# Attention of a hybrid diffusion layer: probabilities computed keys by queries, row sums by ones beside the values, part of the splitting on GpSimd

## The reference, cut to what matters

```python
def one_block(qi):
    s = jnp.einsum("bqkgd,bskd->bkgqs", qi, k).astype(f32) * scale
    p = jax.nn.softmax(s, axis=-1).astype(v.dtype)
    return jnp.einsum("bkgqs,bskd->bqkgd", p, v)
```

## Time and profile before

| what | value |
|---|---|
| median of 3 runs | 2630.91 us (2629.97 to 2631.04) |
| the profiled execution, its own time | 2627.32 us |
| its span, first to last instruction | 2625.6 us |
| PE busy | 2451.6 us, 93% |
| DVE busy | 1925.7 us, 73% |
| ACT busy | 827.6 us, 32% |
| POOL busy | 186.5 us, 7% |
| the attention's loop | from about 1024 to 1299 us of the span |

### The profile page before, as it was taken

The page is one execution under the profiler, slowest core; times in us unless marked ns, Lnnn a source line. Parts: engine busy times, 40 slices in busy tenths (PEclk is TensorE's granted clock), DMA queues, the critical chain, the costliest instruction groups (busy, mean ns, idle before and its releaser), DMA issues. The chain is left out here.

```text
span 2625.6 us, 38449 instructions
## 1 busy us (share of the span) xinstructions
PE 2451.6 (93%) x15508; PEld 1500.0 (57%) x15508; DVE 1925.7 (73%) x2867; ACT 827.6 (32%) x1313; POOL 186.5 (7%) x220
## 2 busy tenths in 40 slices
PE   7999999999999787999799889899899999999987
PEld 2555555555555466777576666545455555555543
DVE  4687777789576766888648658798877676677687
ACT  2411111111121345777644454623222121122220
POOL 0000000000000022222200000311000000000002
PEclk9999999999999889999899999899999999999998
DMA  8133322331212111000120111231211111111001
GB/s 329 49 113 97 97 83 94 97 113 62 67 36 85 63 37 27 1 1 1 31 67 15 42 45 37 69 102 49 65 48 48 48 33 47 48 48 38 26 25 65
DMA packets 151085, 160.55 MB, mean 61 GB/s; under 512 B 11767, under 2 KB 128403, under 8 KB 149922
## 3 DMA queue, kind: packets, MB, share of 16 engines
q1 hardware_dynamic: 150946, 158.61, 19.1%
HBM read 148.47 MB, written 10.12 MB: 60 GB/s over the span
## 5 line engine op out<-in xcount | busy, mean ns | idle before, releaser
L2010 PE MATMUL psum<-act_hi,ffn_win_hi 128*128 128x384 f16 x2064 | 675.2, 327 | 4.8 <-DVE ffn_win_lo L2334 2.4
L2010 PE MATMUL psum<-act_lo,ffn_win_hi 128*128 128x384 f16 x2064 | 674.8, 327 | 0.0
L2010 PE MATMUL psum<-act_hi,ffn_win_lo 128*128 128x384 f16 x2064 | 674.7, 327 | 0.0
L2210 ACT ACTIVATE ffn_silu<-psum,ffn_win_inverse 128x384 f32<-128x384 f32 x132 | 76.3, 578 | 1061.5 <-PE psum L2010 1057.8
L2402 DVE SCALAR_TENSOR_TENSOR Y<-psum,ffn_h_unit,Y 128x512 f32<-128x512 f32 x324 | 239.8, 749 | 108.2 <-PE psum L2055 106.2
L2055 PE MATMUL psum<-ffn_wout_hi,ffn_h_hi 128*128 128x512 f16 x720 | 278.1, 386 | 7.5 <-issue 5.3
L2010 PEld LDWEIGHTS psum<-act_hi,ffn_win_hi 128*128 128x128 f16 x2064 | 202.5, 98 | 139.1 <-DVE ffn_win_lo L2334 2.8
L2010 PEld LDWEIGHTS psum<-act_hi,ffn_win_lo 128*128 128x128 f16 x2064 | 202.5, 98 | 134.7 <-issue 2.0
L2010 PEld LDWEIGHTS psum<-act_lo,ffn_win_hi 128*128 128x128 f16 x2064 | 202.5, 98 | 133.9 <-issue 1.5
L2055 PE MATMUL psum<-ffn_wout_lo,ffn_h_hi 128*128 128x512 f16 x720 | 277.7, 386 | 0.0
L2055 PE MATMUL psum<-ffn_wout_hi,ffn_h_lo 128*128 128x512 f16 x720 | 277.2, 385 | 0.0
(11 more groups left out here) (379 smaller groups left out, 4298.3 us busy)
## 6 DMA issues: line engine op xcount, KB each, us to landing
ffn_win_raw<-in_w_in SPq DMA_DIRECT2D x88, 512.0 KB, 5.1
w_mod<-in_w_mod SPq DMA_DIRECT2D x36, 1024.0 KB, 5.0
ffn_wout_raw<-in_w_out SPq DMA_DIRECT2D x44, 512.0 KB, 4.1
scan_w_raw<-in_w_mix SPq DMA_DIRECT2D x20, 512.0 KB, 5.3
x_after<-Y SPq DMA_DIRECT2D x9, 512.0 KB, 2.6
mixout_residual<-x_after SPq DMA_DIRECT2D x9, 512.0 KB, 3.5
Y<-in_x_sample SPq DMA_DIRECT2D x8, 512.0 KB, 11.6
ffn_residual<-in_x_sample SPq DMA_DIRECT2D x8, 512.0 KB, 3.3
```

The costliest lines, as they stand in the source:

```text
L2010: last = nc.tensor.matmul(bank[:, 0:CH], win[b][w][:, half, k, :], K.A[a][:, k, c * CH:(c + 1) * CH], start=(n == 0), stop=(n == 3 * KT - 1))
L2210: nc.scalar.activation(sa[s][:], pa[s][:, 0:CH], ACT.Silu, scale=winv[:, b:b + 1]).then_inc(silu, 1)
```

## The change

Scores are computed with keys in partitions and the four heads' queries as 512 columns. The product of a tile then comes out as the product with values needs it.

- `main` now computes the queries-by-keys scores from the high part of the queries alone (one product per stretch instead of two), only to find each query's minimum; there is one set of 1280 columns, and `main` waits for the `least` before it, where it used to wait for exponentials. `tails` is gone.
- `score_rows`: four transposes of the minima give rows; ScalarE copies one row to partition 64 of the low tile of the queries, and a second key tile, `k_hi_ones`, has ones there, so that `scores`' second product (65 partitions) adds the row.
- `scores`: two products of 512 columns per key tile, into a rotation of three banks. ScalarE takes the exponential (512 columns) to a ring of four tiles in SBUF and then the high part from there. The low part is subtracted from SBUF too: tiles 1, 3, 5, 7 on GpSimd, the others on VectorE.
- `values`: three products per tile. The first and third have high values and 64 columns of ones as weights, so that the lower 64 output rows are the row sums; the second has the low values (64 columns). Two banks alternate from unit to unit.
- `take_out`: VectorE takes the reciprocal of the 64 x 512 sums and copies the 64 x 512 values out; `low_half`, `add_halves`, `inverses` and `inverse_rows` are gone.
- GpSimd writes the ones by three memsets before the loop. Unit 0's exponentials are no longer in the projection's queue.

The core of the diff:

```diff
@@ Projections.tensor / scalar @@
-        att.tails(pe, 0, 0)
         att.main(pe, 0, 0)
...
-        att.tails(pe, 0, 1)
         att.main(pe, 0, 3)
...
-        act.wait_ge(self.stored, 16 * NT)
-        att.exponents(act, 0, 0)
@@ Attention.main @@
-        if h >= 2:
-            pe.wait_ge(self.ex, h - 1)
...
         if h:
+            pe.wait_ge(self.s_min, h)
+        width = self.tiles[u] * P
+        for a in range(0, width, 512):
+            b = min(a + 512, width)
+            last = self.nc.tensor.matmul(self.S3[:, a:b], self.qT[u % self.NQ][0][:, s * P:(s + 1) * P],
+                                         self.ks[u % NKV][:, key + a:key + b], start=True, stop=True)
+        last.then_inc(self.s_main, 1)
@@ Attention.tensor @@
+            bank, kt, q = self.bank_of(pe, "s", u, n), self.keys(u)[n], self.qT[u % self.NQ]
+            nc.tensor.matmul(bank, self.ks[u % NKV][:, kt * P:(kt + 1) * P], q[0][:], start=True, stop=False)
+            nc.tensor.matmul(bank, self.kr[u % NKV][0:DH + 1, kt * P:(kt + 1) * P], q[1][0:DH + 1, :],
+                             start=False, stop=True).then_inc(self.turned, 1)
...
+            nc.tensor.matmul(bank, with_ones, hi[:], start=(n == 0), stop=False)
+            nc.tensor.matmul(bank[0:DH, :], v[:, 0, :], hi[:], start=False, stop=False)
+            nc.tensor.matmul(bank, with_ones, lo[:], start=False, stop=(n == tiles[u] - 1)).then_inc(self.pv, 1)
...
+        def score_rows(u):
+            pe.wait_ge(self.s_min, (u + 1) * HPK)
...
+                last = nc.tensor.transpose(bank[:, j * P:(j + 1) * P], self.low[:, u % 2, j:j + 1].broadcast_to([P, P]), self.K.ident[:])
...
+        score_rows(0)
         main(pe, 1, 0)
         pe.wait_ge(self.v_lo, 2)
+        pe.wait_ge(self.ones, 3)
...
         for u in range(NU):
+            scores(u, 0)
             values(u - 1, 6)
+            scores(u, 1)
             values(u - 1, 7)
+            main(pe, u + 1, 1)
+            scores(u, 2)
             values(u - 1, 8)
+            scores(u, 3)
             values(u - 1, 9)
             main(pe, u + 1, 2)
+            scores(u, 4)
             values(u, 0)
+            scores(u, 5)
             values(u, 1)
+            main(pe, u + 1, 3)
+            scores(u, 6)
             values(u, 2)
+            self.turn_queries(pe, u + 2)
+            scores(u, 7)
             values(u, 3)
+            score_rows(u + 1)
+            scores(u, 8)
             values(u, 4)
+            scores(u, 9)
             values(u, 5)
             main(pe, u + 2, 0)
@@ Attention.scalar: exponent(u, n + 2) ahead of probs_hi(u, n + 1), through the unit @@
+            nc.scalar.activation(self.pf[g % self.NPF][:], self.bank_at[i], ACT.Exp, scale=-1.0).then_inc(self.ex, 1)
...
+            nc.scalar.activation(self.pt[g % self.NPT][0][:], self.pf[g % self.NPF][:], ACT.Copy).then_inc(self.hi, 1)
@@ Attention.vector @@
+        def take_out(u):
+            dve.wait_ge(self.pv, self.first[u + 1])
             if u:
                 dve.wait_ge(self.scaled, 2 * u)
+            nc.vector.reciprocal(self.rrow[:], self.OB[u % 2][DH:P, :]).then_inc(self.inverse, 1)
+            nc.vector.tensor_copy(self.osum[:], self.OB[u % 2][0:DH, :]).then_inc(self.copied, 1)
...
         for u in range(NU):
+            probs_lo(u - 1, 8)
             probs_lo(u - 1, 9)
+            self.least(dve, u + 1, 1)
             probs_lo(u, 0)
             probs_lo(u, 1)
+            if u:
+                take_out(u - 1)
+            self.least(dve, u + 1, 2)
             probs_lo(u, 2)
             probs_lo(u, 3)
+            self.least(dve, u + 1, 3)
             probs_lo(u, 4)
             probs_lo(u, 5)
+            self.queries_lo(dve, u + 2)
             probs_lo(u, 6)
             probs_lo(u, 7)
...
+            self.least(dve, u + 2, 0)
+        take_out(NU - 1)
@@ Attention.pool @@
+        gp.wait_ge(qkv.q_rstd, NT)
...
+            nc.gpsimd.memset(self.kr[kv][DH:DH + 1, :].bitcast(F32), 1.0).then_inc(self.ones, 1)
...
+        nc.gpsimd.memset(self.vs[:, :, :, 2, :].bitcast(F32), 1.0).then_inc(self.ones, 1)
...
         for u in range(self.NU):
+            probs_lo(u, 1)
...
+            probs_lo(u, 3)
...
+            scaled(u - 1)
+            probs_lo(u, 5)
+            rope(u, 4 if u % 2 else 1)
+            probs_lo(u, 7)
+        scaled(self.NU - 1)
```

More of the change, by code:

```diff
@@ L1038, in __init__ @@
         place = Plan(nc, K.att_at)
[L1039 to L1048, removed]
+        self.ks, self.kr = ([place(f"{n}_{kv}", [P, NKT * P], F32R) for kv in range(NKV)] for n in ("k_stack", "k_hi_ones"))
+        rows, late = Plan(nc, K.h_at), Plan(nc, ring_at + 24576)
+        self.qT = [[(rows if i == 2 else place)(f"qT_{i}_{x}", [P, HPK * P], F32R) for x in ("hi", "lo")] for i in range(self.NQ)]
+        self.pf = [rows(f"probs_{i}", [P, HPK * P]) for i in range(self.NPF)]
+        self.osum = rows("pv_sum", [DH, HPK * P])
+        assert rows.at <= ring_at
+        self.vs = late("v_lo_hi_ones", [P, NKT, NKV, 3, DH], F32R)
+        late.at += 512 + 4096
+        self.rrow = late("inverse_rows", [DH, HPK * P])
+        self.low = late("score_min", [P, 2, HPK])
         assert late.at <= SCAN_RAW_AT
@@ L1081, in full, with score_view @@
         return u < NKV * CTX_T
[L1083 to L1087, removed]
+    def score_view(self, u):
+        return self.S3[:, 0:self.tiles[u] * P]
     def load_scan_weights(self, sp):
@@ L1102, in bank_of @@
         i = self.place_of[x]
-        if i >= 2:
-            kind, u, n = self.order[i - 2]
+        last = [j for j in range(i) if self.bank_at[j] is self.bank_at[i]][-1:]
+        for j in last:
+            kind, u, n = self.order[j]
             if kind == "r":
                 pe.wait_ge(self.rows, u + 1)
-            else:
-                pe.wait_ge(self.lo if kind == "p" else self.in_lo, self.split_at[self.order[i - 2]])
-        return self.T[i % 2]
+            elif kind == "s":
+                pe.wait_ge(self.ex, self.first[u] + n + 1)
+            else:
+                pe.wait_ge(self.in_lo, self.split_at[self.order[j]])
+        return self.bank_at[i]
     def turn_keys(self, pe, kv, b):
@@ L1157, in tails @@
[L1157 to L1162, removed]
-        if h:
-            pe.wait_ge(self.ex, h)
-        self.scores(u, 2 * pair, 1024, 1024, 256)
-        self.scores(u, 2 * pair + 1, 1280, 0, 256).then_inc(self.s_tail, 1)
+        h, key = u * self.HPK + s, self.keys(u)[0] * P
@@ L1185, in values @@
             g = self.first[u] + n
[L1186 to L1192, removed]
-            last.then_inc(self.pv, 1)
@@ L1415, in rope, with probs_lo, scaled @@
                 qkv.rope_query(gp, nc.gpsimd, t, *steps)
-        for u in range(self.NU):
-            if u % 2 == 0:
-                rope(u, 0, 1)
-            else:
-                gp.wait_ge(self.turned, self.place_of["q", u, 0] + 1)
-                rope(u, 2, 3, 4)
-            gp.wait_ge(self.added, u + 1)
-            gp.wait_ge(self.rows, u + 1)
+        def probs_lo(u, n):
+            if u < 0 or n >= self.tiles[u]:
+                return
+            g = self.first[u] + n
+            gp.wait_ge(self.hi, g + 1)
+            nc.gpsimd.tensor_tensor(self.pt[g % self.NPT][1][:], self.pf[g % self.NPF][:], self.pt[g % self.NPT][0][:].bitcast(F32),
+                                    ALU.subtract).then_inc(self.lo_pool, 1)
+        def scaled(u):
+            if u < 0:
+                return
+            gp.wait_ge(self.copied, u + 1)
+            gp.wait_ge(self.inverse, u + 1)
             kt0, t = HGH + 2 * (u % NKV), u // NKV
```

246 lines of the change are left out of this document (106 added, 140 removed).

## The result

| | before | after |
|---|---|---|
| median | 2630.44 us (2629.97 to 2631.04) | 2680.84 us (2675.37 to 2686.07) |
| profiled execution, span | 2625.6 us | 2674.0 us (its own time 2675.71) |
| ratio | | 1.0191, 95% interval 1.0163 to 1.022 |
| mean granted clock of the span | 0.970 | 0.958 |

The change costs 1.9%. I had forecast the sign, the stall and the period, and half of the cost: +25 of span came out as +48.4. The four runs lie in two pairs, near 2675.5 (mean granted clock 0.958) and near 2686 (0.953, by estimate some 27 us more at half clock, which can account for the 10 us), and the profile is of the lower one.

A forecast was written before the change was run, and what follows sets the result against it. PE bounds the loop, with DVE close behind; afterwards PE stalls behind the reciprocal. Opening -5.6, unit 0 -1.4, fourteen periods +20 and end +11.7 sum to +25 us, so 2655, range 2606 to 2680.

The forecast's parts named there:

- PE's slots, 14.9 us a unit: Attention loop: PE's work for a unit of four heads, counted by distances between instructions, sums to 14.9 us.
- The reciprocal, 3.4 us by the slope of the earlier trace: VectorE's 64 x 512 reciprocal in `take_out`: 6.3 ns a column carried to 512 gives 3.4 us.
- The stall of 2.9 and period 17.8: Attention loop: PE stands 2.9 us a unit for the minimum behind `take_out`; period 17.8 us against 16.36.
- The formula 14.4 + D: Loop period in us with D the reciprocal's time; break-even at D = 2.0.
- The opening, -5.6: Before the loop: first values near 1026.7 instead of 1032.31, -5.6 us, bounds 0 and -8.
- The clock stays at 1.00 in the stall: Attention loop: PE keeps full clock through the 2.9 us stall, so no half-clock cost in the sum.
- C: Rival: the clock falls in the loop's stall, +20 to +40 over the main case, 2675 to 2695; chance 0.07.
- my own case: Whole kernel: reciprocal of 3.2 to 4.4 us with the opening's bounds, 2640 to 2677; chance 0.62.
- The end, +11.7: From unit 15's first values to GpSimd's last products: 32.7 us against 21.0, with three reciprocals in a row.
- Rival D: VectorE and GpSimd hinder each other: `probs_lo(u, 0)` ahead of `take_out` waits up to 1.04 us more, 2671; chance 0.06.
- B: Rival, faster: the reciprocal costs what an addition does, D = 0.67, period 15.1, -24 us, 2607; chance 0.16.
- E: Rival, nearly even: D near 2, or small operations exaggerate the slope, 2620 to 2636; chance 0.09, half of it faster.

The follow-up runs named there:

- the spread kernel: Changed kernel with the reciprocal as block transposes plus a 64x16 reciprocal, steps spread over VectorE's queue, GpSimd's scaling behind its last low part: 2619.07 us, ratio 0.9958.
- the copy: Changed kernel with a plain copy of the 64 x 512 sums in place of the reciprocal, division left out: 2628.88 us, ratio 0.9989.
- the short reciprocal: Changed kernel with block transpose, 64x16 reciprocal and transpose back in the old reciprocal's place in the queue: 2632.14 us, ratio 1.0008.
- the kernel with the copy and all low parts on VectorE: Changed kernel with a copy in place of the reciprocal (division left out) and GpSimd's low parts moved to VectorE: 2666.75 us, ratio 1.0144.

## Why the prediction was right or wrong

- **PE's slots, 14.9 us a unit:** right. Unit 0, which has no stall, takes 14.93, and the spread kernel comes down to 15.5.
- **The reciprocal, 3.4 us by the slope of the earlier trace rows:** right, 3.36. Carried from 8 columns to 512, 6.3 ns a column held. The estimate of 4.3 from the repeat count in the Trainium skill (VectorE: DVE Perf Modes, First, the fixed hardware budget) was a quarter too high.
- **The stall of 2.9 and period 17.8:** right, 2.91 and 17.93, and with the stall filled 265.1 us for the loop against 264.1 forecast. The formula 14.4 + D held for D = 1.67 also. At D = 0.69 (the copy) it gives 15.1, and 16.2 in the mean was measured: with the queue in this order another limit is there (the spread kernel gets to 15.5).
- **The opening, -5.6:** it measured -5.5, in part by luck: -3.7 is the change's own, and 1.8 is what runs differ by. The first score tile starts at 1020.87, not 1022.2, but the first values come 5.9 us later, not 4.5, and PE ran at half clock until 1024.8, after it had stood 6.97 us for the ones. My steps had no clock in them here either.
- **The clock stays at 1.00 in the stall:** this is the step that failed. I put my 2.9 between 3.71 and 2.40 of the earlier trace rows, gave C 0.07, and the clock fell in nine of thirteen units. It costs 18.7 us in the loop, measured by filling the stall. C's own number, +20 to +40, 2675 to 2695, is where the kernel came out; its price of 1.35 to 2.7 us per fall was about right too, as units of 19.4 and 20.5 against 17.93 show (1.5 and 2.6), though no row stands behind the 2.7 and 5.4 us at half clock from which I had it; the stretches are 3.4 and 6.9 us long. What I read wrongly is what the 2.40 stands for. It was one gap of many, and the trace of before spoke against it elsewhere. After a gap of 2.38 us behind dense work, in the second feed-forward:

```profile
1853.57 0.50 PE L2010 MATMUL psum<-act_hi,ffn_win_hi 128*128 128x384 f16 x1 [2.38 <-DVE ffn_h_even L2367]
1853.60:1856.00 2.40, 2.40 (x8) 1.12 (x9) 1.34 (x2) 2.40 (x2) 0.00 (x0) 0.50 0.00 0
```

  Over its whole span that trace has 14 gaps of PE of 2.1 to 3.1 us that begin at full clock, and in eight of them the clock is at half 1 us after the gap. By these counts rival C deserved at least as much as my own case.
- **The end, +11.7:** mis-sized; it measured +16.1. The three reciprocals come in the order in which I put them, each later (by 1.8, 3.5 and 4.3 us). In 1310 to 1348 us the granted clock was 0.70, and PE waited 3.65 us for a small minimum until 1330.13, with the clock at half from 1328.5 to 1359.3. With the stalls of the loop filled the end takes 35.4 us in place of 37.1, still with half clock from 1311.4 on; and the last reciprocal waits 0.73 us for GpSimd's product, which I had left out. How much of the rest of the 4.4 us is the clock was not tried by itself.
- **Rival D, the engines in each other's way:** there, but not where I looked. (The rows that I took for it agree only roughly: standing until the other is done would have cost 1021.22 - 1020.83 = 0.39 us there, not 0.26.) In the changed kernel low parts of VectorE take 0.90 in place of 0.68 us and hide beside the stall. Once it is gone TensorE and ScalarE wait for low parts, as the run with the copy shows; that this sets the time is argued, since no run takes the contention away and leaves the rest.
- **Rivals B and E:** the reciprocal's size ruled them out, and B's number was some 22 us too good.

## What to carry to other kernels

When an in-order queue gets a long instruction, ask what stands behind it before asking whether the engine has room: VectorE was 81% busy (146.1 of 180 us), and the same work in four pieces won 47 us, in a smaller form 49, and in a smaller form and spread 62. And when the forecast has the tensor engine standing for some 3 us in every period of a loop, count the half clock as part of the case and not as a rival. Look at all gaps of that size in the old trace, not at one: here eight of 14 had been followed by half clock.

## What the hardware showed that I had not expected

- The clock fell to half after a gap of 2.75 us in nine of thirteen units, and with three gaps of 0.98, 0.44 and 1.15 us close together in every other unit of the kernel with the copy and all low parts on VectorE. It stayed at 1.00 where a unit had one gap of 0.98 us (the short reciprocal) and where PE was filled with useless products. Why it falls in one unit and not in the next stays open.
- Filling a stall of 2.8 us with products that nobody reads made the kernel 18 us faster (medians).
- A block transpose on VectorE takes 0.70 to 0.72 us for 64x512 floats, also where its input is read with a repeated element, about as much as a copy (0.68). With two of them and a reciprocal of 64x16 (0.23 us), 3.36 us become 1.67.
- A VectorE subtraction of 0.67 us took up to 2.98 us beside GpSimd (98 of them: median 0.68, mean 0.90; all 27 of over 0.9 us overlap a GpSimd instruction and end 0.35 to 0.75 us after one ends), and a GpSimd one of 128x512 took 1.27 to 1.74.
